# Five places instead of three for the raw weights of the experts: the end of the arena and the place of the norm's parameters beside the three of before

## The reference, cut to what matters

```python
    for e in range(N_EXPERTS):                                   # 16 experts of width 512
        hid = jax.nn.silu(h @ w_gate[e]) * (h @ w_up[e])
        out = out + gate[..., e:e + 1] * (hid @ w_down[e])
...
        ffn = grouped_moe(h, router_w, router_b, w_gate[i], w_up[i], w_down[i])
        ple = jax.nn.sigmoid(h @ ple_gate[i]) * (p[i] @ ple_proj[i])
        h = layer_norm(DEEPNORM_ALPHA * h + ffn + ple, ln2_g[i], ln2_b[i])
```

## Time and profile before

| | |
|---|---|
| median of 3 runs | 2120.77 us (2118.07 to 2121.94) |
| the profiled execution: time, span | 2126.26 us, 2125.0 us |
| PE busy | 1890.2 us (89%) |
| DVE busy | 1370.0 us (64%) |
| ACT busy | 1146.6 us (54%) |
| mean granted TensorE clock | 0.934 |
| HBM read | 409.47 MB, 194 GB/s over the span |

### The profile page before, as it was taken

How to read it: one execution, slowest core, us unless ns; L and a number is a source line. 1 busy time by engine, 2 the same in 40 slices (tenths; PEclk the granted TensorE clock), 3 DMA queues, 4 the chain that set the end, 5 groups by cost and what they waited for, 6 DMA issues and landing times.

```text
span 2125.0 us, 27386 instructions
## 1 busy us (share of the span) xinstructions
PE 1890.2 (89%) x11220; PEld 1610.0 (76%) x11220; DVE 1370.0 (64%) x1591; ACT 1146.6 (54%) x1576; POOL 155.7 (7%) x152
## 2 busy tenths in 40 slices
PE   4978878888889888888887899999999899999998
PEld 4766757766687776666667679988898778998997
DVE  4576778888756677878876446656556436556555
ACT  3465577777646457767774444434444534444443
POOL 0000202210000012202000000000000000000000
PEclk8899899999899989989998889999999989999999
DMA  7313488888842248878885335554554423654552
GB/s 214 116 60 134 173 300 292 297 314 312 281 138 100 84 159 307 295 288 301 303 306 161 119 99 164 174 198 168 189 196 143 158 81 124 203 190 159 199 181 97
DMA packets 203010, 413.16 MB, mean 194 GB/s; under 512 B 16352, under 2 KB 118496, under 8 KB 186496
## 3 DMA queue, kind: packets, MB, share of 16 engines
q1 hardware_dynamic: 201792, 409.76, 56.6%
q10 hardware_dynamic: 1088, 1.57, 0.3%
HBM read 409.47 MB, written 1.84 MB: 194 GB/s over the span
## 4 chain that ended last, share of the span: by engine, by line
PE 55%; DVE 17%; DMA 13%; ACT 8%; issue 2%; POOL 0%; ACTq 0%; DVEq 0%
DVE weights_lo L367 11%; PE PS L382 9%; PE PS L386 8%; PE PS L383 8%; DMA weights_raw<-in_w_up 8%; PE PS L390 6%; PE PS L393 6%; PE PS L394 6%; ACT weights_hi L362 5%; DMA weights_raw<-in_w_down 4%; PE PS L1350 1%; DMA weights_raw<-in_w_gate 1%; PE PS L1364 1%; PE PS L1367 1%; PE PS L409 1%
## 5 line engine op out<-in xcount | busy, mean ns | idle before, releaser
L367 DVE TENSOR_TENSOR weights_lo<-weights_raw,weights_hi 128x1024 fp32r<-128x1024 f32 x752 | 881.7, 1219 | 320.6 <-ACT weights_hi L362 317.5
L362 ACT ACTIVATE weights_hi<-weights_raw 128x1024 fp32r<-128x1024 f32 x752 | 748.2, 1046 | 247.0 <-PE PS L394 103.1
L382 PE MATMUL PS<-hT_hi,weights_hi 128*128 128x256 f32 (+1 forms) x1488 | 433.1, 291 | 28.3 <-ACT weights_hi L362 18.5
L386 PE MATMUL PS<-hT_hi,weights_lo 128*128 128x256 f32 (+1 forms) x1488 | 429.8, 289 | 2.9 <-DVE weights_lo L367 2.9
L383 PE MATMUL PS<-hT_lo,weights_hi 128*128 128x256 f32 (+1 forms) x1488 | 429.5, 289 | 0.0
L382 PEld LDWEIGHTS PS<-hT_hi,weights_hi 128*128 128x128 f32 (+1 forms) x1488 | 290.7, 195 | 36.9 <-issue 16.5
L386 PEld LDWEIGHTS PS<-hT_hi,weights_lo 128*128 128x128 f32 (+1 forms) x1488 | 290.2, 195 | 4.7 <-DVE weights_lo L367 4.0
L383 PEld LDWEIGHTS PS<-hT_lo,weights_hi 128*128 128x128 f32 (+1 forms) x1488 | 290.6, 195 | 1.9
L390 PE MATMUL PS<-weights_hi,opa_hi 128*128 128x512 f32 x384 | 153.9, 401 | 8.3 <-DVE opa_lo L549 8.1
L393 PE MATMUL PS<-weights_lo,opa_hi 128*128 128x512 f32 x384 | 152.8, 398 | 0.0
L394 PE MATMUL PS<-weights_hi,opa_lo 128*128 128x512 f32 x384 | 152.7, 398 | 0.0
(11 more groups left out here) (318 smaller groups left out, 2965.6 us busy)
## 6 DMA issues: line engine op xcount, KB each, us to landing
weights_raw<-in_w_in SPq DMA_DIRECT2D x80, 1024.0 KB, 5.5
weights_raw<-in_w_gate SPq DMA_DIRECT2D x64, 1024.0 KB, 5.3
weights_raw<-in_w_up SPq DMA_DIRECT2D x64, 1024.0 KB, 7.2
weights_raw<-in_w_down SPq DMA_DIRECT2D x64, 1024.0 KB, 5.9
weights_raw<-in_w_ff SPq DMA_DIRECT2D x64, 1024.0 KB, 5.2
weights_raw<-in_w_branch SPq DMA_DIRECT2D x12, 1024.0 KB, 5.0
weights_raw<-in_w_o SPq DMA_DIRECT2D x8, 1024.0 KB, 4.9
weights_raw<-in_ple_gate SPq DMA_DIRECT2D x8, 1024.0 KB, 7.3
```

The lines of the kernel that those rows point to most:

```text
L362: act.activation(u.flat[0][:, c:e], u.x[:, c:e], ACT.Copy).then_inc(*sig.mark("w_hi", u.u, i))
L367: dve.tensor_tensor(u.flat[1][:, c:e], u.x[:, c:e], u.flat[0][:, c:e].bitcast(F32), ALU.subtract).then_inc(*sig.mark("w_lo", u.u, i))
L382: pe.matmul(o, w[0], x[0], start=start, stop=False)
L386: return pe.matmul(o, w[1], x[0], start=False, stop=stop)
```

## The change

The loads get a table of places. A unit that is not of an expert has the three raw places of before. A unit of an expert has five: also 2048 floats at the end of the arena (11264 to 13312, place 3) and `pslot` (place 4). The expert units near the end of a layer, those with a unit of another kind among the ten from it on, have four, without `pslot`. Of the places that a unit may have it gets the one whose unit is oldest, and it waits for that unit's `w_lo`. Loads to place 3 also wait for the product "mla y" (its arena part is then free), loads to place 4 for the end of the first norm. The parameters of the second norm are loaded ahead of "down 15 0" instead of ahead of "ple gate 10", once the last unit in place 4 has been split. The places of the split weights stay three.

```diff
+        def places():
+            last, found = [None] * (NRAW + 2), []
+            for u, (name, *_) in enumerate(plan):
+                late = of_expert(name) and not all(of_expert(n) for n, *_ in plan[u:u + 10])
+                n = NRAW if not of_expert(name) else NRAW + 1 if late else NRAW + 2
+                place = min(range(n), key=lambda i: -1 if last[i] is None else last[i])
+                found.append((place, last[place]))
+                last[place] = u
+            return found
...
-                self.raw, d = u % NRAW, u % NSPLIT
-                self.x = raw[:, self.raw, 0:size]
+                d = u % NSPLIT
+                self.raw, self.former = raw_place[u]
+                self.x = (raw[:, self.raw, 0:size] if self.raw < NRAW else
+                          (mem(11264, UNIT) if self.raw == NRAW else pslot)[:, 0:size])
...
-            if u.u >= NRAW:
-                sp.wait_ge(*sig.at("w_lo", u.u - NRAW, 1))
+            if u.former is not None:
+                sp.wait_ge(*sig.at("w_lo", u.former, 1))
+            if u.raw >= NRAW:
+                l = int(u.name[-1])
+                sp.wait_ge(*(sig.at("ps", f"mla y {l}") if u.raw == NRAW else sig.at("norm_dve", f"ln1 {l} new1")))
...
-            if name == "ple gate 10":
-                sp.wait_ge(*sig.at("norm_dve", f"ln1 {l} new1"))
+            if name == "down 15 0":
+                late = max(u.u for u in units if u.raw == NRAW + 1 and u.name[-1] == str(l))
+                sp.wait_ge(*sig.at("w_lo", late, 1))
                 norm_params(sp, f"ln2 {l}", a["ln2_g"][l], a["ln2_b"][l])
```

More of the change, by code:

```diff
@@ L322, in build, with of_expert @@
         assert len(place) == len(plan)
+        def of_expert(name):
+            return name.startswith(("gate ", "up ", "down "))
+        def places():
[7 more added lines that the diff above has]
+            return found
+        raw_place = places()
         class Unit:
```

## The result

The changed kernel takes 2054.64 us (median of 4 runs, 2050.80 to 2057.32), the kernel before 2119.42 us beside it (2110.97 to 2121.94): a ratio of 0.9699, 95% interval 0.9668 to 0.9731, or 64.8 us less. The forecast was 2066 us and 55 us less. Two later repeats gave 2054.6 and 2055.05 us.

What follows compares the result with a forecast made beforehand. Bound: the loop "place free, load, split, place free" with three places. Turns -45.2, heads -8.8 and tails -1 sum to -55 us, from 2126.26 profiled to 2071.3, or 2066 us by the median; range 2047 to 2091.

Steps and rivals of the forecast that it cites:

- The ordinary turn: An expert's turn without a pick, 11 of 14 in each layer: 18.2 us, with 17.8 below and 19.0 above.
- the first rival: Experts' turns: the wait only moves to DVE or the three split places; ordinary turns 19.3 us, 2091 us; chance 0.10.
- The turn with a pick: An expert's turn holding a pick, 3 of 14 in each layer: 22.5 us, from 24.41 us for expert 7.
- the case in which the clock is spared: Turns with a pick: the shorter wait also spares PE's low clock, 1.6 us less, 20.9 us.
- The head: Turns of experts 0 and 1 in each layer: ACT's waits for landings go, -4.4 us a layer, -8.8 us together.
- The tail: End of each layer's experts: less late landing, moved norm parameters hidden by full places; -0.5 us a layer, -1 us together.
- The freed front: Ahead of ple gate 10: without the first norm's wait two loads may leave some 20 us earlier; worth nothing.
- Split places and DVE: Experts' turns: the wait moves to DVE, 91% busy, or the split places; turns 19.3 us, 2091 us; chance 0.10.
- The gap at each load: Experts' loads: the queue keeps a gap at each load; at 326 GB/s turns of 19.3 us, 2091 us; chance 0.07.
- The -37 us: Whole kernel: the sum if 1 MiB transfers run at 330 to 340 GB/s, turns 18.5 to 19.1 us, instead of -55.
- Slower by five open loads: Ordinary turns of both layers: five open loads slow the queue below 303 GB/s; at 290 GB/s 2139 us; chance 0.03.
- More than forecast: Experts' turns: 17.8 us ordinary and 20.9 us with a pick, another 18 us less, 2048 us; chance 0.12.

Runs made afterwards that it cites:

- half loads: The kernel before, three places, each load of an expert's unit bringing only the first half of its bytes; 2058.89 us (one run).

## Why the prediction was right, step by step

**The bound before** was read rightly: the loop of a raw place. The half loads and the added places each take it away, by different means, and both arrive at the same turn.

**The ordinary turn** was the term that was off: 18.2 us forecast, 17.58 measured. I took the length of a turn of the trace before over the 17.8 us worked out from DVE's and PE's parts. That measured turn still had late loads of its own, DVE did only 16 instructions in it, and I had written this down against the first rival without applying it to my own number. The construction itself is 0.2 us long. One of its terms explains more than that: six halves follow each other on DVE in 6.90 us, 1.15 us each, where I put in 7.3 us by their mean duration of 1.219. 22 turns by 0.62 us make 13.6 us.

**The turn with a pick**: 22.5 forecast, 21.6 measured, between it and the 20.9 us of the case in which the clock is spared. The clock was spared, 1.00 over such a turn (302.05 to 323.65 us), so it is that case that came, and it was 0.7 us short. 6 by 0.9 us make 5.4 us. With both, the 14 turns of the two layers gave -64.3 us, not -45.2.

**The head** was right: -4.4 forecast. From ACT's first expert split to the first L1633 it is 266.95 - 250.86 = 16.09 us now, and was 271.62 - 250.75 = 20.87 us. Another profile of the change that starts 4 us later (271.26) has the same 16.11 us.

**The tail** was wrong in sign: -0.5 us a layer forecast, +1.9 and +3.1 measured. I had named the 1 MB ahead of down 15 0 and its 2.6 us, and let the full places hide it. This is the step that failed. The places were full, since the load left only when its own came free, and nothing was hidden: the queue ran at a DMA share of 1.02 and 371 GB/s from 519 to 532.4 us, the load landed 3 us later than without the parameters, ACT waited 2.1 to 2.5 us for it, and in-order ACT passed that to expert 14's output. That is near the 2.6 us that I had as the upper end. Twice 2.6 is 5.2 us, and the medians on one chip are 5.3 us apart, an agreement closer than their noise allows to claim. The clock does not explain the growth: in layer 0 the tail before already had these 16 multiplications at 3.32 us, in layer 1 at 2.67.

**The freed front** at nothing was right (271.61 against 271.62 us).

**The sum**: -64.3, -9.5 for two heads and +5.0 for the tails make -68.8 us against -64.8 by the medians. What is between them is within what two executions differ by. The forecast's own errors, 19 us too little gain in the turns and 6 us too much in the tails, made its 55 us. They have opposite signs, so a part of how close the total came is luck.

**The rivals.** Split places and DVE: turns don't reach 19.3 us, yet the row of splits on ACT and DVE is where the kernel ended, only 1.7 us lower. The gap at each load, and the Trainium skill's 330 to 340 GB/s (SBUF — State Buffer, The DMA setup-cost knee): the trace doesn't bear it out as a limit, 339 GB/s was what the changed kernel asked for from 270 to 520 us, and with less work on ACT and DVE the same queue of 1 MB loads moved 370 GB/s over 250 us. The 359 GB/s that I worked out for a full share was too low as well. The -37 us that I gave for turns of 18.5 to 19.1 us belongs to their long end; by 22 ordinary turns they give -48 to -35 us. Slower by five open loads: no sign of it. "More than forecast", 2048 us, was nearer in the turns than the forecast.

**What stays open.** Why the clock falls in one tail and not in another with the same chain ahead of it (15.79, 17.05 and 18.25 us) was not settled. Nor was a version tried that shortens ACT's row alone, or one that evens out ACT and DVE, for example by giving POOL a part of a split.

## What to carry to other kernels

A ring of buffers is the bound when the chain of waits is one place going round: add places until the landing waits are gone and stop there, since here the fourth did nearly all and the fifth nothing that the medians show. Work the new turn out from the in-order rows of each engine, and prefer that to a measured turn that still holds some of the waits which the change removes. A small load put in front of the last ones of a burst is not free because buffers are full: look at what stands behind the waiting instruction in its engine's order.

## What the runs showed of the hardware

With up to five loads of 1 MB open, landing took a median of 6.7 to 7.8 us from 270 to 520 us, where with three it took 5.3 to 7.6, and this cost nothing. The queue kept 370 GB/s over 250 us and 389 GB/s over 17.5 us, at a DMA share of 0.99 and 1.00; a turn of 16.1 us moves 6.29 MB, 391 GB/s. And 16 small multiplications of PE took 1.74 to 1.75 us at a granted clock of 1.00 and 3.32 us at 0.50, a difference as large in a tail as the late landing itself.
